# Three layer norms that leave weight and bias to the turned tiles, and 512-column up products, in a two-block transformer kernel

## The chip, the cores and the metric

The kernel runs on one core of a Trainium2 chip. The metric is the device time of one execution in microseconds (us). Times come in runs of the whole kernel; one execution was profiled, and all rows below are from it.

## The reference

Batch 1, 256 tokens, width 1024, float32. A first block (adaptive norm, a mixer of two attentions, an MLP) is followed by two layers, each of them a mixer and an MLP with a layer norm behind each:

```
x = first_block(x, c, ...)                       # its MLP: D_FF 4096, square(relu(h @ w1)) @ w2
for i in range(2):
    mix = nsa_pool_mixer(x, ...) if i == 0 else gla_mixer(x, ...)
    x = layer_norm(ALPHA * x + mix, ln1_g[i], ln1_b[i])
    x = layer_norm(ALPHA * x + square(relu(x @ w1[i])) @ w2[i], ln2_g[i], ln2_b[i])
layer_norm(x, g, b) = (x - mean) * rsqrt(var + 1e-5) * g + b      # mean and var over the 1024 channels
```

So there are three MLPs and four layer norms. The norms are numbered 0 to 3 here; norm 0 stands ahead of MLP 1, norm 1 ahead of the second layer's mixer (its input products, "C in"), norm 2 ahead of MLP 2, and norm 3 gives the output.

## The kernel before

Every weight comes from memory once, as tiles of 128 rows x 1024 numbers in six `raw` slots, in one fixed order, fetched by SyncE. For precision each weight tile is split in two: ScalarE copies it to `whi` (rounded to float32r), VectorE writes the rest, `wlo = raw - whi`; both have six slots. Activations are split the same way, `hT_hi` and `hT_lo`, `uhi` and `ulo`. Each product is made of three: hi x hi, hi x lo, lo x hi. `hi_to(s)` and `lo_to(s)` in the programs of ScalarE and VectorE mean: split the weight tiles up to s. A raw slot is free for the next fetch when `wlo` is written (`raw_done`), a split slot when TensorE has used it (`w_used`). All order on an engine is written out by hand: a wait holds everything behind it on that engine.

**Norms.** `x` is two tiles (t = 0, 1) of 128 tokens x 1024. VectorE adds the product to x in halves (`ln_half`, with `bn_stats`), then `ln_end` aggregates, hands the variance to GpSimd (`rsqrt`, a power), and meanwhile and afterwards makes two passes over each half of x: `(x - mean) * g`, then `* rstd + b`. Each half counts up `src_ready`, which releases one quarter: TensorE turns it (4 transposes of 128x128 into PSUM), ScalarE copies it to `hT_hi` (`quarter_hi`), VectorE writes `hT_lo = PSUM - hT_hi` (`quarter_lo`, `hTlo_done`), and the first products wait for that. `busy(b, n)` is n idle-time filler products on TensorE with no use for the result.

**MLP** (`mlp`, 16 steps of 256 of the 4096 inner channels). Step 0 is made with tokens as rows (`up_first`) and turned back (`turn_first`); for steps 1 to 15 `up(j)` makes 256 channels x 256 tokens in one PSUM bank: per 128 channels of the input and per 128 output channels three products of 256 columns (lines 1894 to 1896), 48 in all. Then ScalarE takes relu and its square (`uhi`), VectorE the square again and `ulo`. `down(j)` adds u x w2 to four output banks with 24 products of 512 columns (lines 1752 to 1754, the helper `three`). The order on TensorE is up(j+1), down(j). At the end it is up(14), down(13), up(15) and then the last parts of `down`.

Of the kernel before, what the change touches and what calls it, by code (L numbers as in the profile page):

```python
# [5 lines left out]
F32 = mybir.dt.float32  # L6
# [6 lines left out]
P = 128  # L13
# [157 lines left out]
def block_program(nc, dram, out):  # L171
    with ExitStack() as ctx:
# [3 lines left out]
        def sem(name):  # L176
# [7 lines left out]
        hT_hi = sb("hT_hi", [P, KC, S], F32R)  # L184
        hT_lo = sb("hT_lo", [P, KC, S], F32R)
# [11 lines left out]
        tab = sb("tab", [P, 1536])  # L197
        identb = sb("identb", [P, P], BF16)
# [10 lines left out]
        qkgain = sb("qkgain", [64, 3])  # L209
        bfor = sb("bfor", [P, 8])  # L210
# [55 lines left out]
        x_upd = sem("x_upd")  # L266

        relu_done, uhi_done, ulo_done, usq, up_mm, up_tr = [sem(n) for n in (
            "relu_done", "uhi_done", "ulo_done", "usq", "up_mm", "up_tr")]
# [46 lines left out]
        NF = len(GRP)  # L316
        S_BANK = [0, 1, 0, 1, 0, 1] + [1] * 12
# [25 lines left out]
        T_LAST = {1: T_OUT, 7: T_COUT}  # L343

# [10 lines left out]
        def _(sp):  # L355
# [53 lines left out]
            def fetch_mlp(w1, w2, s0):  # L409
# [22 lines left out]
                for k, f in enumerate([down(13, 0), down(13, 1), up(15, 0), up(15, 1),  # L432
                                       down(14, 0), down(14, 1), down(15, 0), down(15, 1)]):
                    fetch_w(s0 + MLP_TILES - 8 + k, *f)
# [30 lines left out]
        def _(pool):  # L465
# [48 lines left out]
            load_ln(0)  # L514
            rsqrt(S_N2, 1)
# [31 lines left out]
            pool.wait_ge(src_ready, units(6))  # L547
# [3 lines left out]
            pool.wait_ge(src_ready, units(7))  # L551
# [5 lines left out]
            pool.wait_ge(src_ready, units(9))  # L557
# [8 lines left out]
        def _(act):  # L566
# [31 lines left out]
            def quarter_hi(n, q):  # L598
# [3 lines left out]
                if n in T_LAST and in_hT(n, j):  # L602
                    act.wait_ge(w_used, T_LAST[n])
                nc.scalar.activation(split_dst(n, j)[0][:, :, rows_of(t)],
# [19 lines left out]
            def mlp(m, s0):  # L624
# [9 lines left out]
                def relu(j, i=None):  # L634
                    n = j0 + j
                    at = lambda v, d: v if i is None else i * d + v
                    used = s0 + (2 + 2 * j if j < 2 else 4 * j)
                    act.wait_ge(w_used, at(used, 4 * TURN))
                    if n >= 1:
                        act.wait_ge(usq, at(n, TURN))  # L640
                        act.wait_ge(uhi_done, at(n, TURN))
# [6 lines left out]
                for t in range(NT):  # L648
# [6 lines left out]
                    ins = nc.scalar.activation(pr[:, 0, t * FFB:(t + 1) * FFB], AT[:, 2 * t, 0:FFB], ACT.Relu)  # L655
                ins.then_inc(relu_done, 1)
# [3 lines left out]
                relu(1)  # L660
                with act.Fori(0, TURNS) as i:
                    for q in range(TURN):
                        for k in range(4):
                            hi(8 + 4 * q + k, i)
                        relu(2 + q, i)
                nxt[0] = s0 + MLP_TILES - 8
                hi_to(s0 + MLP_TILES - 5)
                relu(MLP_STEPS - 2)
                hi_to(s0 + MLP_TILES - 1)
                relu(MLP_STEPS - 1)  # L670
# [323 lines left out]
            for q in range(4):  # L994
                hi_to(T_CIN + 1 + q) if q in (1, 2) else None
                quarter_hi(6, q)
# [76 lines left out]
        def _(dve):  # L1073
# [66 lines left out]
            def quarter_lo(n, q):  # L1140
# [3 lines left out]
                hi, lo = split_dst(n, j)  # L1144
                tt(lo[:, :, rows_of(t)], tr_bank(n, t, j).rearrange("p (c s) -> p c s", c=4),
# [36 lines left out]
            def ln_half(n, pb, t, h, s_end):  # L1182

                product_wait(pb, t, h, s_end)
                xs = x[:, t, half(h)]
# [4 lines left out]
            def ln_end(n, t, between=None):  # L1190
# [3 lines left out]
                ts(stat[:, c:c + 1], bn[:, t, 13:14], LN_EPS, None, ALU.add).then_inc(var_ready, 1)  # L1194
                dve.wait_ge(ld_row, 32 * (n + 1))
# [7 lines left out]

            def out_norm(n, pb, s_end, stage):
# [5 lines left out]
                lo_to(s_end[1] + 1)  # L1210
                ln_end(n, 0)
# [7 lines left out]
            def mlp(m, s0):  # L1219
# [9 lines left out]
                def square(j, i=None):  # L1229
                    n = j0 + j  # L1230
                    at = lambda v: v if i is None else i * TURN + v
                    dve.wait_ge(relu_done, at(n + 1))
                    if n >= 1:
                        dve.wait_ge(ulo_done, at(n))
                    tt(pr[:, 1, :], pr[:, 0, :], pr[:, 0, :], ALU.mult).then_inc(usq, 1)  # L1235
                    dve.wait_ge(usq, at(n + 1))
                    dve.wait_ge(uhi_done, at(n + 1))
                    tt(ulo[:, j % 2, :], pr[:, 1, :], uhi[:, j % 2, :].bitcast(F32), ALU.subtract).then_inc(ulo_done, 1)
# [3 lines left out]
                dve.wait_ge(relu_done, j0 + 1)  # L1242
# [4 lines left out]
                lo_to(s0 + 7)  # L1247
                square(1)
                with dve.Fori(0, TURNS) as i:
                    for q in range(TURN):  # L1250
                        for k in range(4):
                            lo(8 + 4 * q + k, i)
                        square(2 + q, i)
                nxt[0] = raw_of(s0 + MLP_TILES - 8)
                lo_to(s0 + MLP_TILES - 5)
                square(MLP_STEPS - 2)
                lo_to(s0 + MLP_TILES - 1)
                square(MLP_STEPS - 1)
# [1245 lines left out]
```

## Time and profile before

| | |
|---|---|
| median of 3 runs | 1003.92 us (1003.64 to 1007.0) |
| profiled execution, its own time | 1002.46 us |
| its span in the profile | 1000.3 us |
| TensorE busy / VectorE busy / ScalarE busy | 965.0 / 650.7 / 465.7 us |
| mean granted TensorE clock | 0.994 |

A busy share is an average over stages. What a change is worth is read from the stretch in which it lies: in the MLP stretches TensorE has no idle time, between them it waits.

### The profile page before, as it was taken

The page shows a single profiled execution, that of the slowest core. Times are in us where ns is not written, and L with a number is a line of the kernel's source. Part 1 is how long each engine was busy: PE and PEld are TensorE (multiplying, and loading weights), DVE is VectorE, ACT ScalarE, POOL GpSimd, SP SyncE. Part 2 cuts the span into 40 slices and gives each one's busy share as a digit, 9 for nine tenths or more (in the row PEclk, how much of TensorE's full clock was granted, in tenths as well). Part 3 has the DMA queues.
Part 4 walks back from the last instruction along what each step waited for, and adds up shares of the span by engine and source line. Part 5 has one row for each costly group of instructions (what it writes and reads, how often), then busy time and mean ns, then how long its engine had stood idle before and what let it go on. Part 6 is the DMA issues. An engine that isn't in the chain of part 4 may idle for free.

```text
span 1000.3 us, 15011 instructions
## 1 busy us (share of the span) xinstructions
PE 965.0 (96%) x5664; PEld 828.0 (83%) x5664; DVE 650.7 (65%) x822; ACT 465.7 (47%) x706; POOL 53.9 (5%) x59
## 2 busy tenths in 40 slices
PE   8999999799999999999899999998999999999996
PEld 6778877699999987876699999997776889999995
DVE  5877897875554766566975545557633876555555
ACT  5576535455444444543354445434552435444540
POOL 3040101100000001000200000001000010000000
PEclk9999999999999999999999999999999999999998
DMA  9979778495566557321385565564442547565531
GB/s 309 344 226 304 233 229 274 163 330 176 170 199 202 206 190 167 122 85 53 115 262 188 195 200 174 174 200 152 127 147 85 170 133 244 192 198 199 168 126 43
DMA packets 109991, 186.94 MB, mean 187 GB/s; under 512 B 8696, under 2 KB 67088, under 8 KB 109920
## 3 DMA queue, kind: packets, MB, share of 16 engines
q1 hardware_dynamic: 104800, 177.33, 54.5%
q0 software_dynamic: 2592, 8.53, 3.0%
q8 instruction: 35, 0.57, 0.2%
q10 hardware_dynamic: 2544, 0.35, 0.2%
q14 instruction: 20, 0.16, 0.0%
HBM read 185.13 MB, written 1.05 MB: 186 GB/s over the span
## 4 chain that ended last, share of the span: by engine, by line
PE 79%; DVE 10%; ACT 3%; issue 3%; DMA 2%; POOL 2%; SPq 0%; POOLq 0%; DVEq 0%; ACTq 0%
PE PJ L1752 14%; PE PJ L1753 14%; PE PJ L1754 13%; PE AT L1896 9%; PE AT L1895 9%; PE AT L1894 9%; DVE wlo L1100 2%; POOL rstd L471 2%; PE AT L1983 1%; ACT whi L585 1%; DMA raw<-in_w_out_dram 1%; PE AT L1738 1%; DVE acc L1126 1%; PE AT L1995 1%; DVE bn L1188 1%
## 5 line engine op out<-in xcount | busy, mean ns | idle before, releaser
L1100 DVE TENSOR_TENSOR wlo<-raw,whi 128x1024 fp32r<-128x1024 f32 x144 | 172.9, 1221 | 51.5 <-ACT whi L585 50.6
L1894 PE MATMUL AT<-hT_hi,whi 128*128 128x256 f32 x720 | 203.8, 283 | 0.0
L1896 PE MATMUL AT<-hT_hi,wlo 128*128 128x256 f32 x720 | 203.7, 283 | 0.0
L1895 PE MATMUL AT<-hT_lo,whi 128*128 128x256 f32 x720 | 203.7, 283 | 0.0
L1226 DVE TENSOR_TENSOR wlo<-raw,whi 128x1024 fp32r<-128x1024 f32 x144 | 169.8, 1221 | 32.1 <-ACT whi L632 31.4
L585 ACT ACTIVATE whi<-raw 128x1024 fp32r<-128x1024 f32 x144 | 147.0, 1055 | 51.2 <-DMA raw<-in_w_in_dram 29.1
L1752 PE MATMUL PJ<-whi,uhi 128*128 128x512 f32 x432 | 170.1, 394 | 0.4 <-DVE ulo L1575 0.2
L1753 PE MATMUL PJ<-wlo,uhi 128*128 128x512 f32 x432 | 168.6, 390 | 0.0
L1754 PE MATMUL PJ<-whi,ulo 128*128 128x512 f32 x432 | 168.2, 389 | 0.0
L632 ACT ACTIVATE whi<-raw 128x1024 fp32r<-128x1024 f32 x144 | 144.3, 1049 | 47.5 <-PE PJ L1754 43.9
L1894 PEld LDWEIGHTS AT<-hT_hi,whi 128*128 128x128 f32 x720 | 138.0, 192 | 1.6
L1895 PEld LDWEIGHTS AT<-hT_lo,whi 128*128 128x128 f32 x720 | 138.0, 192 | 1.6
L1896 PEld LDWEIGHTS AT<-hT_hi,wlo 128*128 128x128 f32 x720 | 138.0, 192 | 0.0
L1235 DVE TENSOR_TENSOR pr<-pr 128x512 f32<-128x512 f32 x45 | 31.1, 691 | 162.0 <-ACT pr L642 162.0
L1752 PE MATMUL PJ<-whi,hT_hi 128*128 128x512 f32 (+1 forms) x320 | 131.3, 410 | 4.3 <-DVE hT_lo L1568 1.4
L1754 PE MATMUL PJ<-whi,hT_lo 128*128 128x512 f32 (+1 forms) x320 | 123.9, 387 | 0.0
L1753 PE MATMUL PJ<-wlo,hT_hi 128*128 128x512 f32 (+1 forms) x320 | 123.9, 387 | 0.0
L642 ACT ACTIVATE pr<-AT 128x512 f32<-128x512 f32 x45 | 26.9, 597 | 190.9 <-PE AT L1896 190.9
L1752 PEld LDWEIGHTS PJ<-whi,uhi 128*128 128x128 f32 x432 | 81.3, 188 | 17.8 <-issue 2.0
L1754 PEld LDWEIGHTS PJ<-whi,ulo 128*128 128x128 f32 x432 | 81.1, 188 | 17.4
L1753 PEld LDWEIGHTS PJ<-wlo,uhi 128*128 128x128 f32 x432 | 81.3, 188 | 15.2 <-issue 0.2
L1752 PEld LDWEIGHTS PJ<-whi,hT_hi 128*128 128x128 f32 x320 | 60.5, 189 | 22.1 <-issue 6.1
(312 smaller groups left out, 1061.5 us busy)
## 6 DMA issues: line engine op xcount, KB each, us to landing
raw<-in_mlp_w_dram SPq DMA_DIRECT2D x128, 512.0 KB, 4.9
raw<-in_w_in_dram SPq DMA_DIRECT2D x32, 512.0 KB, 6.3
raw<-in_w_ada_dram SPq DMA_DIRECT2D x32, 512.0 KB, 5.4
raw<-in_w_mlp_in_dram SPq DMA_DIRECT2D x32, 512.0 KB, 5.0
raw<-in_w_mlp_out_dram SPq DMA_DIRECT2D x32, 512.0 KB, 5.1
raw<-in_c_w_in_dram SPq DMA_DIRECT2D x24, 512.0 KB, 4.3
raw<-in_w_ada_dram SPq DMA_DIRECT2D x32, 256.0 KB, 6.4
raw<-in_a_w_in_dram SPq DMA_DIRECT2D x12, 512.0 KB, 5.2
```

Source lines behind the costliest of these rows:

```text
L585: nc.scalar.activation(whi[:, s % SPL, :], raw_slot(r), ACT.Copy).then_inc(hi_done, 1)
L632: nc.scalar.activation(whi[:, s % SPL, :], raw_slot(r), ACT.Copy).then_inc(hi_done, 1)
L642: nc.scalar.activation(pr[:, 0, :], AT[:, j % 2, :], ACT.Relu).then_inc(relu_done, 1)
L1100: tt(wlo[:, n % SPL, :], raw_slot(r), whi[:, n % SPL, :].bitcast(F32), ALU.subtract).then_inc(raw_done, 1)
L1226: tt(wlo[:, s % SPL, :], raw_slot(r), whi[:, s % SPL, :].bitcast(F32), ALU.subtract)\
L1235: tt(pr[:, 1, :], pr[:, 0, :], pr[:, 0, :], ALU.mult).then_inc(usq, 1)
L1752: mm(o, a, hi, start=start, stop=False)
L1753: mm(o, a, lo, start=False, stop=False)
L1754: return mm(o, b, hi, start=False, stop=stop)
L1894: mm(o, whi[:, s % SPL, c], hT_hi[:, k, :], start=first, stop=False, skip_group_check=True)
L1895: mm(o, whi[:, s % SPL, c], hT_lo[:, k, :], start=False, stop=False, skip_group_check=True)
L1896: ins = mm(o, wlo[:, s % SPL, c], hT_hi[:, k, :], start=False, stop=last, skip_group_check=True)
```

## The change

It has four parts.

1. **Up products.** `hT_hi` and `hT_lo` of one input channel block stand side by side, so `whi x hT_hi` and `whi x hT_lo` become one product of 512 columns, each into a half of a bank of its own; `wlo x hT_hi` stays one of 256. An `up` step now has 16 products of 512 columns and 16 of 256, and takes two banks. The two halves of a bank have to be added: ScalarE copies the one out, VectorE adds the other, then takes relu times itself, ScalarE copies the result to `uhi`, VectorE makes `ulo`. One weight tile's `wlo` (11+4q) moves into the middle of that. Step 15's u goes into a free part of `hT`, and the order at the end is up(14), up(15), down(13).
2. **Norms 0 to 2.** VectorE makes one pass over a half: `(x - mean) * rstd`, then `src_ready`. Weight and bias are put on by ScalarE from the turned tile, where a channel is a partition: four activations of 128x128 with scale and bias by partition, into `sc`, and then the rounding copy to `hT_hi`. VectorE subtracts from `sc`.
3. **x itself** still needs weight and bias for the next residual: `affine`, two passes over each of the four halves (8 instructions on VectorE for each norm), behind `square(1)` of MLP 1 and 2 and among the first C-in tiles.
4. **Small orders.** GpSimd loads the three weights and biases by channel (`lncol`, six transfers of 1024 single numbers) ahead of `rsqrt(S_N2)`; fillers ahead of MLP 1 and 2 go from 1+2+4 to 1+2, at C in by one each; the weight splits T_CIN+2 and +3 stand at other places.

```diff
-        hT_hi = sb("hT_hi", [P, KC, S], F32R)
-        hT_lo = sb("hT_lo", [P, KC, S], F32R)
+        hT = sb("hT", [P, KC, 2, S], F32R)
+        hT_hi, hT_lo = hT[:, :, 0, :], hT[:, :, 1, :]
...
             load_ln(0)
+            for n in range(3):
+                g, b = (("ln1_g_2", "ln1_b_2"), ("ln2_g_2", "ln2_b_2"))[n % 2]
+                for i, v in enumerate((g, b)):
+                    pool.dma_start(lncol[:, 2 * n + i, :], dram[v][n // 2].rearrange("(k p) -> p k", p=P),
+                                   allow_slow_non_contiguous=True).then_inc(ld_col, 16)
             rsqrt(S_N2, 1)
...
+                if n in LN_STAGE:
+                    act.wait_ge(ld_col, 96)
+                    if q >= 2:
+                        act.wait_ge(hTlo_done, units(n) + q - 1)
+                    for c in range(4):
+                        ins = nc.scalar.activation(turned_y(q)[:, c, :], tr_bank(n, t, j)[:, c * P:(c + 1) * P], ACT.Identity,
+                                                   scale=lncol[...], bias=lncol[...])
+                    link(ins)
+                    nc.scalar.activation(split_dst(n, j)[0][:, :, rows_of(t)], turned_y(q), ACT.Copy).then_inc(hThi_done, 1)
+                    return
...
-                    nc.scalar.activation(pr[:, 0, :], AT[:, j % 2, :], ACT.Relu).then_inc(relu_done, 1)
-                    act.wait_ge(relu_done, at(n + 1, TURN))
-                    nc.scalar.activation(uhi[:, j % 2, :], pr[:, 0, :], ACT.Square).then_inc(uhi_done, 1)
+                    nc.scalar.activation(pr[:, 0, :]..., AT[:, up_banks(j), S:], ACT.Copy).then_inc(cross_out, 1)
+                    act.wait_ge(usq, at(n + 1, TURN))
+                    nc.scalar.activation(u_slot(j)[0], blocks4(pr[:, 1, :]), ACT.Copy).then_inc(uhi_done, 1)
...
+                if n < 3:
+                    between()
+                    rstd_wait()
+                    for j in range(2):
+                        xs = x[:, t, half(j)]
+                        ts(xs, xs, bn[:, t, 12:13], rstd[:, c:c + 1], ALU.subtract, ALU.mult).then_inc(src_ready, 1)
+                    return
...
+            def affine(n, stage, t, j):
+                dve.wait_ge(ld_row, 32 * (n + 1))
+                dve.wait_ge(tr_done, units(stage) + 2 * t + j + 1)
+                xs = x[:, t, half(j)]
+                link(tt(xs, xs, rows[:, 0, half(j)], ALU.mult))
+                tt(xs, xs, rows[:, 1, half(j)], ALU.add).then_inc(x_new, 1)
...
+                    z = pr[:, 0, :].rearrange("p (f s) -> p f s", f=2)
+                    tt(z, AT[:, up_banks(j), 0:S], z, ALU.add).then_inc(up_out, 1)
+                    dve.wait_ge(up_out, at(n + 1, TURN))
+                    stt(pr[:, 1, :], pr[:, 0, :], 0.0, pr[:, 0, :], ALU.max, ALU.mult).then_inc(usq, 1)
+                    between() if between else None
...
-            lo_to(T_CIN + 1)
-            for t in range(NT):
-                ln_half(1, B_MLP1, t, 0, (T_CIN, T_CIN))
-                ln_half(1, B_MLP1, t, 1, (T_CIN, T_CIN))
-                lo_to(T_CIN + 3) if t else None
-                ln_end(1, t)
-                quarter_lo(6, 2 * t)
-                quarter_lo(6, 2 * t + 1)
-                lo_to(T_CIN + 2)
+            lo_to(T_CIN)
+            ln_half(1, B_MLP1, 0, 0, s_end)
+            ln_half(1, B_MLP1, 0, 1, s_end)
+            ln_end(1, 0, lambda: lo_to(T_CIN + 1))
+            ln_half(1, B_MLP1, 1, 0, s_end)
+            quarter_lo(6, 0)
+            quarter_lo(6, 1)
+            ln_half(1, B_MLP1, 1, 1, s_end)
+            ln_end(1, 1, lambda: lo_to(T_CIN + 2))
+            lo_to(T_CIN + 3)
+            quarter_lo(6, 2)
+            quarter_lo(6, 3)
...
-                                mm(o, whi[:, s % SPL, c], hT_hi[:, k, :], start=first, stop=False, skip_group_check=True)
-                                mm(o, whi[:, s % SPL, c], hT_lo[:, k, :], start=False, stop=False, skip_group_check=True)
-                                ins = mm(o, wlo[:, s % SPL, c], hT_hi[:, k, :], start=False, stop=last,
+                                mm(o, whi[:, s % SPL, c], hT[:, k, :, :].rearrange("p a s -> p (a s)"),
+                                   start=k == 0, stop=False, skip_group_check=True)
+                                ins = mm(o[:, 0:S], wlo[:, s % SPL, c], hT_hi[:, k, :], start=False, stop=k == KC - 1,
                                          skip_group_check=True)
```

## Rows read from the trace of the kernel before

**Rows 1.** The page: the shares of the chain that ended last, by engine.

```profile
PE 79%; DVE 10%; ACT 3%; issue 3%; DMA 2%; POOL 2%; SPq 0%; POOLq 0%; DVEq 0%; ACTq 0%
```

**Rows 2.** Busy time by stretch: length, PE, PEld, DVE, ACT, POOL, clock, DMA.

```profile
418.00:421.50 3.50, 3.50 (x11) 2.69 (x11) 1.78 (x5) 1.91 (x9) 0.00 (x0) 0.59 0.13 49
...
516.00:666.00 150.00, 150.00 (x973) 137.55 (x972) 82.25 (x81) 67.86 (x79) 0.00 (x0) 1.00 0.60 198
```

**Rows 3.** Timeline of TensorE, one step of MLP 1: start, duration, line, shape.

```profile
560.16 0.28 PE L1894 MATMUL AT<-hT_hi,whi 128*128 128x256 f32 x1
...
565.91 0.40 PE L1752 MATMUL PJ<-whi,uhi 128*128 128x512 f32 x1
...
571.38 0.28 PE L1894 MATMUL AT<-hT_hi,whi 128*128 128x256 f32 x1
```

**Rows 4.** Groups by line and form: count, busy us, mean ns, idle before.

```profile
L644 ACT ACTIVATE uhi<-pr 128x512 fp32r<-128x512 f32 x45 | 28.6, 634 | 1.4
L604 ACT ACTIVATE hT_hi<-AT 128x512 fp32r<-128x512 f32 x24 | 13.9, 596 | 67.5 <-PE AT L1738 67.5
L655 ACT ACTIVATE pr<-AT 128x256 f32<-128x256 f32 x6 | 2.3, 381 | 6.7 <-PE AT L1754 6.7
...
L1180 DVE TENSOR_TENSOR x<-x,sc 128x512 f32<-128x512 f32 x8 | 5.5, 692 | 0.3
L1119 DVE TENSOR_SCALAR prT<-raw,cvec 128x512 f32<-128x512 f32 x3 | 1.4, 479 | 0.0
```

**Rows 5.** Timeline of VectorE and TensorE, norm 0 to MLP 1.

```profile
496.80 0.75 DVE L1201 SCALAR_TENSOR_TENSOR x<-x,rstd,rows 128x512 f32<-128x512 f32 x1 [0.52 <-POOL rstd L471]
...
497.61 0.66 PE L1738 MATMUL AT<-cst,x 128*128 128x128 f32 x4 [0.26 <-DVE x L1201]
...
499.74 0.60 PE L1738 MATMUL AT<-cst,x 128*128 128x128 f32 x4
...
501.79 0.35 PE L1752 MATMUL AT<-whi,hT_hi 128*128 128x256 f32 x1
...
503.30 0.28 PE L1894 MATMUL AT<-hT_hi,whi 128*128 128x256 f32 x1
...
509.72 0.47 PE L1752 MATMUL PJ<-whi,uhi 128*128 128x512 f32 x1
```

**Rows 6.** Timeline of ScalarE: activations with scale and bias by partition.

```profile
16.66 0.60 ACT L709 ACTIVATE hT_hi<-qT,modc 128x256 fp32r<-128x256 f32 x1
17.17 0.58 ACT L712 ACTIVATE pr<-qT,modc 128x256 f32<-128x256 f32 x1
```

**Rows 7.** Timeline of TensorE and VectorE, norm 2 to MLP 2.

```profile
819.57 0.60 PE L1873 MATMUL AT<-cst,pr 128*128 128x128 f32 x4
...
823.11 0.47 PE L1752 MATMUL PJ<-whi,uhi 128*128 128x512 f32 x1
...
827.65 4.62 DVE L1226 TENSOR_TENSOR wlo<-raw,whi 128x1024 fp32r<-128x1024 f32 x4
```

**Rows 8.** Timeline of VectorE and TensorE, norm 1 to C in.

```profile
681.63 0.68 DVE L1186 SCALAR_TENSOR_TENSOR x<-x,PJ 128x512 f32<-128x512 f32 x1
...
684.52 1.23 DVE L1100 TENSOR_TENSOR wlo<-raw,whi 128x1024 fp32r<-128x1024 f32 x1
...
677.11 0.66 PE L1738 MATMUL AT<-cst,x 128*128 128x128 f32 x4 [1.19 <-DVE x L1201]
...
681.80 0.58 PE L1752 MATMUL PJ<-whi,hT_hi 128*128 128x512 f32 x1
...
690.23 0.58 PE L1752 MATMUL PJ<-whi,hT_hi 128*128 128x512 f32 x1
```

**Rows 9.** Timeline of GpSimd; and a step of the chain that ended last.

```profile
181.10 1.48 POOL L471 TENSOR_TENSOR rstd<-stat,nhalf 128x1 f32<-128x1 f32 x1 [16.10 <-DVE stat L1157]
...
379.86 1.68 POOL L528 DMA_DIRECT2D acc<-in_a_cmp_pos_dram  x1
...
164.28 8.67 DMA raw<-in_w_out_dram
```

More of the change, by code:

```diff
@@ L550, in _ @@
                 rsqrt(S_LN + 2 + t, 1)
[L551 removed]
+            pool.wait_ge(x_new, 8)
             load_ln(2)
@@ L659, in mlp @@
                 hi_to(s0 + 7)
-                relu(1)
+                square_hi(1)
                 with act.Fori(0, TURNS) as i:
@@ L1246, in mlp @@
                 tt(ulo[:, 0, :], AT[:, 3, :], uhi[:, 0, :].bitcast(F32), ALU.subtract).then_inc(ulo_done, 1)
-                lo_to(s0 + 7)
-                square(1)
+                lo_to(s0 + 6)
+                square(1, between=lambda: lo_to(s0 + 7))
+                for t in range(NT):
+                    for j in range(2):
+                        affine(*((0, 5), (2, 8))[m - 1], t, j) if m else None
                 with dve.Fori(0, TURNS) as i:
                     for q in range(TURN):
-                        for k in range(4):
+                        for k in range(3):
                             lo(8 + 4 * q + k, i)
-                        square(2 + q, i)
+                        square(2 + q, i, lambda: lo(11 + 4 * q, i))
                 nxt[0] = raw_of(s0 + MLP_TILES - 8)
-                lo_to(s0 + MLP_TILES - 5)
-                square(MLP_STEPS - 2)
+                lo_to(s0 + MLP_TILES - 7)
+                square(MLP_STEPS - 2, between=lambda: lo_to(s0 + MLP_TILES - 6))
+                lo_to(s0 + MLP_TILES - 4)
+                square(MLP_STEPS - 1, between=lambda: lo_to(s0 + MLP_TILES - 3))
                 lo_to(s0 + MLP_TILES - 1)
-                square(MLP_STEPS - 1)
             nc.vector.memset(rows[:, 0, 0:S], 0.0).then_inc(zeroed, 1)
@@ L1900, in down_part @@
                 def down_part(j, s, f, t, h, first=False, last=False):
-                    c = slice(f * S + t * P, f * S + (t + 1) * P)
+                    hi, low = u_slot(j)
                     w = slice(512 * h, 512 * (h + 1))
-                    return three(bank(pb + h, t), uhi[:, j % 2, c], ulo[:, j % 2, c], whi[:, s % SPL, w],
+                    return three(bank(pb + h, t), hi[:, 2 * f + t, :], low[:, 2 * f + t, :], whi[:, s % SPL, w],
                                  wlo[:, s % SPL, w], first, last)
@@ L1919, in down @@
                         ins.then_inc(w_used, 1)
+                transposes(stage, 1, src)
                 busy(3, 1) if m else None
-                transposes(stage, 1, src)
+                up_first(0, 0)
                 busy(3, 2) if m else None
-                up_first(0, 0)
-                busy(3, 4) if m else None
                 transposes(stage, 2, src)
@@ L1938, in mlp @@
                 up(14, 54)
-                down(13, 56)
-                up(15, 58)
+                up(15, 56)
+                down(13, 58)
                 if spare:
+                    pe.wait_ge(up_out, j0 + MLP_STEPS - 1)
                     spare()
```

88 lines of the change are left out of this document (49 added, 39 removed).

## The prediction

> **What bounds the kernel now.** I read the page first, then busy time by stretch, then timelines where TensorE waits. The chain that ended last is TensorE for 79% [rows 1]. In a stretch of MLP 1, TensorE is busy 150.00 of 150.00 us; VectorE has 82 and ScalarE 68 [rows 2]. So inside the three MLPs only TensorE's own work counts. Ahead of MLP 1, of C in and of MLP 2 it waits for a serial chain: VectorE norms a half, TensorE turns it, ScalarE rounds it, VectorE makes the low part. There, latencies count.
>
> **Up products.** From 560.16 to 565.91 run the 48 products of an up step, 0.1198 us each; from 565.91 to 571.38 the 24 of a down step, 0.2279 us each [rows 3]. At 2.4 GHz 256 columns last 0.1067 us and 512 last 0.2133, so each product pays some 0.013 us beside its columns. The new step has 16 of either: 16 x (0.2279 + 0.1198) = 5.56 us against 5.75, 0.187 less. The shape of 512 is at hand in `down`, from the same kind of operand, so I take its spacing. Bounds: no gain, if the joined product costs two of 256 (0.2396); 0.21 per step, if it saves one whole overhead of 0.013. 42 steps (j = 2 to 15) stand in TensorE's unbroken stream: **-7.9 us**. Step 1 of each MLP is left out, for a wait behind it decides (below).
>
> The Trainium skill (TensorE: Matmul & The Clock Gate, Back-to-back issue gap) gives columns/2.4 plus only 2.5 ns. The rows disagree: 0.1198 and 0.2279 us. By the page's figure the 42 steps would save an estimated 1.7 us.
>
> The longer way to u is covered. Behind up(j): copy out 0.60, add 0.69, relu times itself 0.69, copy 0.63, subtract 0.69 [rows 4], with one weight split of 1.2 in it: some 5 us. `down(j)` starts only after down(j-1) and up(j+1), 5.47 + 5.56 = 11.0 us later. VectorE's step grows from 6.0 to 6.7 us of 11.0, ScalarE's hardly. If that cover were gone, each step would pay the excess. The new order at the end hides step 15's chain under down(13); it was hidden before.
>
> **The norm's release.** Before, two passes a half. Now VectorE restarts at the same place after GpSimd (496.80, [rows 5]), with one pass of 0.48 (L1119, [rows 4]; upper bound 0.75, L1201 [rows 5]). The quarter is released 0.25 us earlier, and the fourth, which waited for two more passes, some 2 us earlier.
>
> **The price in ScalarE.** `quarter_hi` was one copy of 0.60 (L604). Now four activations, 128 columns, two per-partition operands. With 256 columns these start 0.51 us apart [rows 6]; 256 columns less cost 0.596 - 0.381 = 0.215 us [rows 4], 128 columns 0.11. So 0.40 apart, 1.7 us for four, then a rounding copy of 0.63 (L644): 2.3 us, **1.7 more per quarter**. Bounds: 0.9 more, if the operands cost nothing (0.381 - 0.107 for one, overlapped by 0.08), and 2.0, if they don't overlap. ScalarE takes quarters in turn, so a second one follows 2.3 us behind the first.
>
> *Norm 0 to MLP 1.* The first half: released 0.27 us earlier, 1.7 us longer on ScalarE. VectorE waits for it with `quarter_lo(0)` ahead of the second half's sums; that uses up the gain of the passes, and the second variance is out at the same time as before. Third quarter: VectorE's pass 496.80 to 497.28, turned at 497.36, low part done near 501.1. The fourth is turned by 500 but queues on ScalarE: 2.3 us later. Before, turned at 499.74, used at 501.79, 2.05 us [rows 5]. Now `up_first(1, 1)` starts at 497.36 + 2.1 + 1.7 + 2.2 = 503.4, 1.6 later. The wait behind `turn_first` (819.57 to 823.11 in MLP 2, 3.54 us [rows 7]) hangs on the middle of up(1), now at 2.78 rather than 2.88 us: down(0) comes **1.5 us later** than 509.72. The fewer fillers cost and give nothing: TensorE would have waited.
>
> *Norm 2 to MLP 2.* The same, but VectorE here ran `lo_to` (1.2 us) before the first variance and now runs it under GpSimd's power: 0.7 us off the start. **0.8 us later.**
>
> *Norm 1 to C in.* VectorE drops one weight split ahead of the first sums: variance 0.64 earlier, first transposes at 676.2 instead of 677.11, the second quarter right behind, TensorE ready at 679.3. First quarter's low part: first product at 680.0 against 681.80 [rows 8]. But T_CIN+2's split, done by 681.63 before [rows 8], now stands behind both quarters' low parts, the sums of the second half (half of 681.63 to 684.52, 1.44 us [rows 8]) and the variance: second quarter rounded at 681.4, low part 682.2, sums 683.5, split 683.8 to 685.1. TensorE has used T_CIN and +1 by 682.7 and **waits 2.4 us**. T_CIN+3 follows at 687.2, and t = 0 ends near 688.6. Only then are the last quarters turned; from there 2.05 + 1.7 us: second tile at 692.3 against 690.23. **2.1 us later.** Nothing behind gives it back, for TensorE is the bound there too.
>
> **`affine`.** 8 passes of 0.69 (L1180, [rows 4]), pairs of 1.33: 5.3 us a norm. At C in there is room between splits. In MLP 1 and 2 they stand ahead of tile 8's split, behind `square(1)`: that was at 827.65 [rows 7], 4.54 us after down(0)'s start; now it is square 0.6 us later, and 5.3: 10.5 us after, done at 11.7. TensorE needs it after down(0) and up(2), 5.57 + 5.56 = 11.1. **Stall 0.7 us, twice** (0 to 1.5).
>
> **GpSimd.** Six more transfers ahead of a power that waited 16.10 us for its operand [rows 9]. One with 4096 single numbers took 1.68 us to issue [rows 9]; six with 1024 at 0.5 to 1.7 are 3 to 10 us, hidden. They share the DMA engines with a weight tile that is on the chain with 8.67 us (from 164.28, [rows 9]). Between 0 and 1.6 us; I take 0.2.
>
> **Sum.** -7.9 + 1.5 + 0.8 + 2.1 + 1.4 + 0.2 = -1.9 us. Against the profiled execution's 1002.46 that is 1000.6; the median of the runs lies 1.46 above it, so I predict **1002.0**.
>
> **Rivals.** (A) *The turned tiles are as quick as before.* Operands by partition cost little, and C in's split order costs less than I think. For it: without a price for the operands a quarter is longer by 0.9 us only, and the release is up to 2 us earlier. Against: the spacing with operands [rows 6]. The transitions then cost some 1 us in all, stalls included: -7, 997.0.
>
> (B) *The joined products give nothing or little.* A 512-column product into an AT bank, between two of 256, could cost two of them, by its weight load. Against: `down` shows 0.2279 with a load each. The sum becomes +6.0, 1009.9: slower. It passes +5 us once the joined product costs over 0.238 us. By the Trainium skill's 2.5 ns (same page and section) an estimate is +4.3, just short of that.
>
> (C) *The clock falls.* From 418.0 to 421.5 the granted clock was 0.59 on average [rows 2], so a part of it ran at 1.2 GHz instead of 2.4; such a dip costs a busy TensorE 3.5 x 0.41 = 1.4 us. C in gets waits of 2.4 and 2.3 us within 10 us of each other. Two dips more: 1004.8. Against: the waits before, up to 1.19 us [rows 8], brought none there. [...]
>
> (D) *The small loads delay the weight tile* by the whole 1.6 us: 1003.4.
>
> **Chances.** Forecast 0.48, A 0.30, B 0.08, C 0.09, D 0.05. A measurement here tells 0.5% (5 us) from no change. Faster by over that, below 998.9: most of A, a little of the forecast, 0.30. Slower, above 1008.9: B and a tail, 0.10. Within: 0.60. The forecast's own bounds (quarters 0.9 to 2.0, stalls 0 to 1.5, loads 0 to 1.6) give 998 to 1006; with A, 995.5 to 1006.5.
>
> **What would show it.** Right: up steps of 5.56 us, steps of 11.03 us, TensorE still without idle in the MLPs; ScalarE's four activations 0.4 us apart; `up_first(1, 1)` waiting for ScalarE; at C in a wait of 2.4 us for VectorE's `wlo`; 0.7 us ahead of down(1). Wrong: another spacing of the joined product, quarters of 1.5 us on ScalarE, or waits inside the loops, where VectorE or a weight fetch comes late.

## The result: 6 us slower

The changed kernel takes 1011.16 us (median of 6 runs, 1010.37 to 1014.59) against 1004.97 for the kernel before (6 runs): a ratio of 1.0065 with a 95% interval of 1.0049 to 1.0081, so 4.9 to 8.1 us slower. I had predicted 1002.0.

The execution profiled is the slowest of the six, 1014.59 us with a span of 1012.8. The page of after has these rows, the chain's shares among them (that of before in [rows 1]):

```profile
PE 967.6 (96%) x4924; PEld 793.3 (78%) x4924; DVE 675.7 (67%) x879; ACT 479.4 (47%) x754; POOL 60.1 (6%) x65
...
PE 74%; DVE 10%; ACT 5%; DMA 5%; issue 4%; POOL 2%; SPq 0%; POOLq 0%; DVEq 0%; ACTq 0%
```

TensorE's share of the chain fell from 79 to 74%, and the DMA's rose from 2 to 5%, for which my sum had no more than the 0.2 us of the small loads.

**A step of MLP 1**, on the timeline of after (start, duration, line, shape), against [rows 3]:

```profile
569.94 0.39 PE L1947 MATMUL AT<-hT,whi 128*128 128x512 f32 x1
...
570.28 0.40 PE L1947 MATMUL AT<-hT,whi 128*128 128x512 f32 x1
570.51 0.28 PE L1949 MATMUL AT<-hT,wlo 128*128 128x256 f32 x1
570.63 0.40 PE L1947 MATMUL AT<-hT,whi 128*128 128x512 f32 x1
570.87 0.28 PE L1949 MATMUL AT<-hT,wlo 128*128 128x256 f32 x1
570.99 0.40 PE L1947 MATMUL AT<-hT,whi 128*128 128x512 f32 x1
...
575.58 0.40 PE L1809 MATMUL PJ<-whi,uhi 128*128 128x512 f32 x1
```

The up step lasts 575.58 - 569.94 = 5.64 us, not 5.56: 0.11 less than before, where I had 0.187. From a joined product to the start of the product of 256 behind it are 0.23 to 0.24 us (0.2358 on the mean of the 212 pairs between 529 and 684 us), from a product of 256 to the next joined one 0.117.

**Norm 0 to MLP 1**, against [rows 5]: timeline of ScalarE and TensorE.

```profile
499.35 1.50 ACT L623 ACTIVATE sc<-AT,lncol 128x128 f32<-128x128 f32 x4 [5.90 <-PE AT L1795]
...
500.88 0.63 ACT L627 ACTIVATE hT<-sc 128x512 fp32r<-128x512 f32 x1
...
501.42 1.49 ACT L623 ACTIVATE sc<-AT,lncol 128x128 f32<-128x128 f32 x4
...
519.31 0.48 PE L1809 MATMUL PJ<-whi,uhi 128*128 128x512 f32 x1 [0.16 <-issue]
...
531.05 0.50 PE L1809 MATMUL PJ<-whi,uhi 128*128 128x512 f32 x1 [0.36 <-DVE wlo L1268]
```

A quarter occupies ScalarE for 2.07 us (499.35 to 501.42; I had 2.3). down(0) starts at 519.31, 9.59 us after its place before. The norm's first transposes were 8.24 late already, so the norm itself costs 1.35 us. At down(1) TensorE waits for the weight tile that stands behind `affine`; the wait and its after-effect make some 0.6 us (see `affine` in the table of terms).

**Norm 1 to C in**, against [rows 8]: TensorE's first transposes and its waits.

```profile
685.36 1.11 PE L1795 MATMUL AT<-cst,x 128*128 128x128 f32 x8 [0.77 <-DVE x L1228]
694.04 0.47 PE L1809 MATMUL PJ<-whi,hT 128*128 128x512 f32 x1 [1.92 <-DVE wlo L1124]
696.52 0.50 PE L1809 MATMUL PJ<-whi,hT 128*128 128x512 f32 x1 [0.86 <-DVE wlo L1124]
701.69 0.47 PE L1809 MATMUL PJ<-whi,hT 128*128 128x512 f32 x1 [2.21 <-DVE hT L1170]
```

Here are the waits that I had drawn: 1.92 us for the third weight tile (I had 2.4), 2.21 for the last quarters (I had 2.3).

**The small loads.** GpSimd's timeline, and the piece of the chain that ended last which answers to [rows 9]:

```profile
168.61 0.92 POOL L527 DMA_DIRECT2D lncol<-in_ln_g_dram  x1
...
173.01 0.88 POOL L527 DMA_DIRECT2D lncol<-in_ln_b_dram  x1
...
169.03 14.56 DMA raw<-in_w_mlp_in_dram
```

Six issues of 0.9 us, and a weight tile that is on the chain for 14.56 us. The tile on the chain before, with 8.67, was another; but the four tiles `raw<-in_w_mlp_in` issued between 150 and 195 us land after a median of 14.7 us here and of 9.6 before.

### The profile page after: what moved, and what is told of

It reads as the page before. It is cut to its first block, busy times and chain, and to the rows that moved or that the text cites. A ratio compares the mean times of both kernels' runs of the same rounds, so it can differ in the third digit from the quotient of the medians.

```text
span 1012.8 us, 13660 instructions
## 1 busy us (share of the span) xinstructions
PE 967.6 (96%) x4924; PEld 793.3 (78%) x4924; DVE 675.7 (67%) x879; ACT 479.4 (47%) x754; POOL 60.1 (6%) x65
## 4 chain that ended last, share of the span: by engine, by line
PE 74%; DVE 10%; ACT 5%; DMA 5%; issue 4%; POOL 2%; SPq 0%; POOLq 0%; DVEq 0%; ACTq 0%
PE AT L1947 16%; PE PJ L1809 14%; PE PJ L1810 13%; PE PJ L1811 13%; PE AT L1949 8%; DVE wlo L1124 2%; DMA raw<-in_w_in_dram 2%; POOL rstd L480 2%; DMA raw<-in_w_mlp_in_dram 1%; PE AT L2036 1%; ACT sc L623 1%; ACT whi L599 1%; PE AT L1795 1%; DVE acc L1150 1%; PE AT L2048 1%
## 5 line engine op out<-in xcount | busy, mean ns | idle before, releaser
L1947 PE MATMUL AT<-hT,whi 128*128 128x512 f32 x720 | 256.2, 398 | 0.0
L1949 PE MATMUL AT<-hT,wlo 128*128 128x256 f32 x720 | 202.1, 281 | 0.0
L1947 PEld LDWEIGHTS AT<-hT,whi 128*128 128x128 f32 x720 | 135.3, 188 | 32.8
L1810 PE MATMUL PJ<-wlo,uhi 128*128 128x512 f32 x408 | 159.2, 390 | 0.0
L1809 PE MATMUL PJ<-whi,hT 128*128 128x512 f32 (+1 forms) x344 | 144.2, 419 | 14.4 <-DVE wlo L1124 6.2
L1278 DVE TENSOR_TENSOR pr<-AT,pr 128x512 f32<-128x512 f32 x45 | 31.1, 690 | 160.8 <-ACT pr L665 160.8
L1949 PEld LDWEIGHTS AT<-hT,wlo 128*128 128x128 f32 x720 | 136.0, 189 | 1.5
L1810 PE MATMUL PJ<-wlo,hT 128*128 128x512 f32 (+1 forms) x344 | 136.4, 396 | 0.0
L1811 PE MATMUL PJ<-whi,hT 128*128 128x512 f32 (+1 forms) x344 | 136.1, 396 | 0.0
L1809 PEld LDWEIGHTS PJ<-whi,hT 128*128 128x128 f32 x344 | 67.2, 195 | 35.2 <-issue 11.5
L1811 PEld LDWEIGHTS PJ<-whi,hT 128*128 128x128 f32 x344 | 67.0, 195 | 14.3
L1810 PEld LDWEIGHTS PJ<-wlo,hT 128*128 128x128 f32 x344 | 67.3, 196 | 13.0 <-issue 1.0
```

Source lines behind the costliest of these rows:

```text
L1278: tt(z, AT[:, up_banks(j), 0:S], z, ALU.add).then_inc(up_out, 1)
L1809: mm(o, a, hi, start=start, stop=False)
L1810: mm(o, a, lo, start=False, stop=False)
L1811: return mm(o, b, hi, start=False, stop=stop)
L1947: mm(o, whi[:, s % SPL, c], hT[:, k, :, :].rearrange("p a s -> p (a s)"), start=k == 0, stop=False, skip_group_check=True)
L1949: ins = mm(o[:, 0:S], wlo[:, s % SPL, c], hT_hi[:, k, :], start=False, stop=k == KC - 1, skip_group_check=True)
```

## Where the time went, by stretch

The groups that the helper `transposes` makes on TensorE, and the turns of `turn_first`, are the same in all kernels, so the starts of their first products cut each profile into like stretches (us; each is a difference of two starts, and the last ends with TensorE's last product). Transposes by other lines are no landmarks. "Before" was profiled three times.

| stretch | before, 3 profiles | after |
|---|---|---|
| start to the first group of transposes | 135.01, 136.61, 136.06 | 138.64 |
| to MLP 0's first transposes | 48.42, 48.44, 48.80 | 52.16 |
| to MLP 0's turn | 15.44, 15.45, 15.83 | 16.94 |
| MLP 0, from its turn | 171.30, 171.30, 171.31 | 169.75 |
| second attention | 120.25, 121.93, 118.75 | 121.16 |
| norm 0 to its turn | 15.77, 15.75, 15.75 | 17.12 |
| MLP 1, to C in's transposes | 170.93, 170.92, 170.92 | 169.59 |
| C in, to the helper's next group | 100.66, 100.67, 100.65 | 105.38 |
| to MLP 2's turn | 41.80, 41.80, 41.79 | 42.22 |
| MLP 2 to the end | 171.40, 171.38, 171.38 | 170.48 |

The MLPs and the norms repeat within 0.02 us. In the first 200 us and in the second attention the same kernel scatters by up to 3 us, since the granted clock falls at changing places. Two such places of after, in the view of busy time by stretch (columns as in [rows 2]):

```profile
418.00:425.00 7.00, 7.00 (x46) 6.60 (x46) 2.36 (x4) 3.39 (x12) 0.00 (x0) 0.76 0.54 148
...
701.00:708.00 7.00, 6.31 (x21) 5.06 (x22) 5.34 (x7) 4.69 (x8) 0.00 (x0) 0.76 0.25 72
```

A mean of 0.76 over 7 us is 7 x 0.24 x 2 = 3.4 us at 1.2 GHz, and costs a busy TensorE 1.7 us. The first lies in the second attention, where before has one as well [rows 2]; the second, in C in, is in none of the three profiles of before. (I had priced such a fall at 1.4 us, from a window that began 0.6 us inside it.) The profile that I predicted from has the shortest start of the three.

## The experiments

**1. The loads moved behind; the loads alone.** The first takes the changed kernel and issues the six loads later on GpSimd's queue:

```diff
             load_ln(0)
-            for n in range(3): ... pool.dma_start(lncol[:, 2 * n + i, :], ...)
             rsqrt(S_N2, 1)
...
+            for n in range(3): ... pool.dma_start(lncol[:, 2 * n + i, :], ...)
             for t in range(NT):
                 rsqrt(S_LN + t, 1)
```

> The changed kernel with its six loads of lncol issued behind GpSimd's loads for the second attention (near 380 us, used from 490 us). Theory 1 (the six loads at 168 to 174 us hold up a weight tile, 3.8 us of TensorE's time): 3.8 us less than the changed kernel, so 1007.4, 2.4 us above before; the weight tiles raw<-w_mlp_in land in some 9.6 us as before, not 14.7. Rival (the 3.8 us between 165 and 183 us is the scatter of one execution, such as a dip of the clock): no change, 1011.2, 6.2 above before.

The second adds the `+` lines to the kernel before, between `load_ln(0)` and `rsqrt(S_N2, 1)`:

> The kernel before, with the six loads of lncol added at the changed kernel's place, into a tile that nothing reads. Theory 1: 3.8 us above before, 1008.8, all of it between 165 and 183 us. Rival: within 0.5 us of before.

Measured: 1009.21 us (12 runs; ratio to before 1.0043, 1.0024 to 1.0062) and 1007.47 us (12 runs; 1.0029, 1.0012 to 1.0046). So the loads alone cost the kernel before 1.2 to 4.6 us (theory 1 had 3.8), and moving them gave 2 us. The transfers of 170 to 180 us, by slices of 0.25 us, in before, then in the kernel before with the loads:

```profile
GB/s 328 344 295 320 291 287 246 352 324 348 328 361 389 385 389 381 377 369 393 369 401 320 381 361 365 389 397 356 410 373 356 369 352 393 406 340 410 352 442 365
```

```profile
DMA  9998998999999999999999499668999999999899
GB/s 344 401 442 328 385 451 360 459 401 393 426 401 393 401 385 340 300 252 106 74 66 33 45 34 62 72 131 170 204 154 183 129 168 137 183 214 247 246 303 307
```

The rate falls from some 370 to between 33 and 215 GB/s for over 4 us, while the engines' busy share (the digits, in tenths) is under 0.8 in three slices only. The loads are 96 packets of 256 bytes in this trace, beside 96 of 4 bytes. From 174 to 179.5 us a packet of 256 bytes took 0.32 us on the mean, where one of 4096 took 0.16, and the weight tiles' packets of 1024 took 0.094 us instead of the 0.049 that they take in before from 170 to 173 us. The stretch from 165 to 183 us lasted 18.6 to 18.9 us in nine of the ten profiles without the loads at that place (19.6 in the tenth) and 20.7, 21.0 and 21.1 with them (22.3 in that of after, where the clock stood at 1.2 GHz for some of it): 2.2 us. The 20.99 among them had the clock down for its last 1.1 us only, so the 2.2 us are not the clock's; the rest of theory 1's 3.8 us goes with the fall in after's profile, as its rival had it. The Trainium skill (DMA: Bandwidth & Descriptors, Rules for kernel authors) says that a last dimension that isn't contiguous becomes one descriptor per element. The trace agrees in that 24 KB cost the others so much, but it records packets and not descriptors, and no run loads the same 24 KB contiguously: that single numbers are the reason, and not six more small loads, is argued.

**2. The product alone; the MLPs alone.** The changed kernel with the joined product taken apart:

```diff
-  mm(o, whi[:, s % SPL, c], hT[:, k, :, :].rearrange("p a s -> p (a s)"), start=k == 0, ...)
+  mm(o[:, 0:S], whi[:, s % SPL, c], hT_hi[:, k, :], start=k == 0, stop=False, ...)
+  mm(o[:, S:], whi[:, s % SPL, c], hT_lo[:, k, :], start=False, stop=k == KC - 1, ...)
```

> The changed kernel with each joined product of 512 columns taken apart into two of 256 into the two halves of the same bank; nothing else differs. Theory 2 (the joined product has a spacing of 0.236 us, so a step gains 0.11 us): 45 steps of 0.11, 5 us above the changed kernel, 1016.1. Rival (my forecast, 0.187 a step, the rest being a disturbance of one execution): 8.4 us above it. Second rival (the joined product gains nothing): the same time.

The other way round, the MLPs of after in the kernel before:

```diff
 # from the changed kernel: hT, up_banks, u_slot, square_hi, square, up, down_part, the order at the end
 # from the kernel before: ln_end, out_norm, quarter_hi, quarter_lo, C in, the fillers; no affine, no lncol
```

> The kernel before with the MLPs of the changed one: the joined products, the longer way to u, the new order at the end; the three norms, their quarters, the loads and the fillers as before. Theory 2: 5 us under before, 1000.0, since nothing but the steps of 0.11 us remains. Rival (0.187 a step): 8 us under it, 997. Second rival (the longer way to u costs waits of its own in the MLPs): at or above before.

Measured: 1014.11 us (1.0091, 1.0065 to 1.0117) and 1005.39 us (12 runs; 0.9999, 0.9980 to 1.0017). In the profiles the joined products are worth what theory 2 says: with them apart, MLP 0 lasts 171.33 us against 169.75; the MLPs alone in the kernel before last 169.81, 169.03 and 169.83, 4.9 us less in all. Of the 1.9 us in MLP 1, 0.33 is not TensorE's work: from its last product to the next transposes are 1.25 us instead of 1.58. But the time of that kernel didn't fall by 5 us, and the split one rose by 3 only. Something outside the MLPs took 2 to 5 us back in the kernels that have the joined products. One piece is in the profile of the MLPs alone: a fall of the clock in C in, 101.92 us instead of 100.66.

**3. Two more profiles of before, to know the scatter.**

> The kernel before itself, for one more profile of it. The execution first profiled showed two falls of the granted clock beside the one at its end, and a mean of 0.994; the mean over 29 executions is 0.989. Theory 3 (falls at changing places in the first 200 us belong to every execution and not to an edit): four to six falls here, the first transposes of 165 us some 2 to 5 us later than in the first profile, and from 205 us on the same lengths of every stretch within 0.1 us, one fall near 418 us apart. Rival (the edits bring the early falls): as in the first profile, two.

> The same once more: the scatter of the first 200 us between two executions of one kernel on one chip. Theory 3: up to 4 us between the two; the stretch from 165 to 183 us within 1 us of 18.55 us in both, since no small loads are there.

Measured: 1005.75 and 1002.73 us, spans 1003.6 and 1000.6; the clock fell four times in the one and twice in the other, beside the fall at the end. Every stretch behind 205 us but the second attention repeats (table above). The scatter of falls is real, but the first stretch of after is longer than all three.

**4. Joined products in groups.** In the kernel of the MLPs alone, one weight tile's products in two groups:

```diff
+                        for part in range(2):
                             for kk in range(4):
                                 for f in range(2):
...
+                                    if part == 0:
                                         mm(o, whi[:, s % SPL, c], hT[:, k, :, :]...)
+                                    else:
                                         ins = mm(o[:, 0:S], wlo[:, s % SPL, c], hT_hi[:, k, :]...)
```

> The MLPs of the changed kernel in the kernel before, with the products of each weight tile in two groups: its eight joined products of 512 columns first, then its eight of 256 columns. Theory 2a (the joined product's 0.236 us comes from the alternation of 512 and 256 columns): 0.227 and 0.120 us, 5.55 us a step, 0.09 us less than in the changed kernel, 45 steps: 4 us under the alternating form. Rival (it is the joined product's operands or its bank): 0.236 us as before, and then 5.64 us a step; if the spacing of the 256 rises from 0.117 to 0.120 as well, 5.7 us.

Measured: 998.24 us; 0.9943, 0.9923 to 0.9963. Timeline of one step (a row with x8 is eight in a row):

```profile
603.47 1.98 PE L1905 MATMUL AT<-hT,whi 128*128 128x512 f32 x8
...
605.28 1.11 PE L1908 MATMUL AT<-hT,wlo 128*128 128x256 f32 x8
606.23 2.00 PE L1905 MATMUL AT<-hT,whi 128*128 128x512 f32 x8
608.07 1.12 PE L1908 MATMUL AT<-hT,wlo 128*128 128x256 f32 x8
609.03 0.40 PE L1764 MATMUL PJ<-whi,uhi 128*128 128x512 f32 x1
```

609.03 - 603.47 = 5.56 us, to the hundredth what I had predicted for the changed kernel. The same product with the same operands into the same bank is 0.227 to 0.229 us behind another of 512 columns. Theory 2a holds: the alternation costs 0.008 us a joined product and gives 0.003 back on the product of 256. Against the alternating form of experiment 2 the MLP stretches are 3.4 us shorter (168.65, 168.00 and 168.67 us); the two kernels' ratios lie 5.6 us apart, and the rest is outside the MLPs.

The grouped order also changes the bank at every product, which the alternating one doesn't. That is not the reason: three products in a row go into one bank in `down`, at 0.228, and in before's `up`, at 0.120. And a single change of size costs nothing in sum. In before, the first product of a `down` (512 behind 256 columns) takes 0.233 us in all 13 cases between 520 and 660 us, and the first of an `up` (256 behind 512) takes 0.113: 0.006 more and 0.007 less. In the grouped kernel a product of 512 that has one of 512 in front takes 0.227 also where one of 256 follows. So it is not what follows that sets the spacing, and only the strict alternation leaves 0.006 us a pair.

**5. The third weight tile at C in.** First, in the kernel of experiment 1 (loads behind), its low part under GpSimd's power:

```diff
-            hi_to(T_CIN + 1)
+            hi_to(T_CIN + 2)
...
-            lo_to(T_CIN)
+            lo_to(T_CIN + 1)
...
-            ln_end(1, 0, lambda: lo_to(T_CIN + 1))
+            ln_end(1, 0, lambda: lo_to(T_CIN + 2))
...
-            ln_end(1, 1, lambda: lo_to(T_CIN + 2))
-            lo_to(T_CIN + 3)
+            ln_end(1, 1, lambda: lo_to(T_CIN + 3))
```

> The changed kernel with the six loads behind and, at C in, the third weight tile split ahead of the first quarters: ScalarE rounds it before the first quarter, VectorE makes its low part under GpSimd's first power, the fourth tile's under the second power. Theory 4 (TensorE's wait of 2.0 us there hangs on that split): the wait for wlo goes from 2.8 us to under 1, the variance of the first half is 0.64 us later, and from the first transposes to the end of C in the stretch is 1.5 to 2 us shorter than the 3.1 us more than before. Rival (the second quarters decide, so that the gain is given back there): 0.5 us or less.

Measured: 1009.10 us (one run). C in is 2.57 us shorter than with the loads behind alone (101.21 against 103.78), but MLP 1's stretch 2.16 longer (171.77 against 169.61): 0.41 in all, the rival. The timeline shows why:

```profile
681.19 1.06 ACT L599 ACTIVATE whi<-raw 128x1024 fp32r<-128x1024 f32 x1 [6.27 <-PE PJ L1810]
682.28 1.22 DVE L1124 TENSOR_TENSOR wlo<-raw,whi 128x1024 fp32r<-128x1024 f32 x1 [2.33 <-ACT whi L599]
683.42 1.00 DVE L1228 TENSOR_SCALAR x<-x,bn,rstd 128x512 f32<-128x512 f32 x2
684.02 1.11 PE L1794 MATMUL AT<-cst,x 128*128 128x128 f32 x8 [2.93 <-DVE x L1228]
```

ScalarE can round that tile only when TensorE lets go of its slot (six tiles back), at 681.19. VectorE had nothing else to go on with, and the norm's passes stood behind. The wait moved from behind the transposes to ahead of them.

So the low part belongs where VectorE is idle anyway, between the second half's first sums and the first quarter. The changed kernel with the loads behind, the groups of experiment 4, and:

```diff
-            hi_to(T_CIN + 1)
+            hi_to(T_CIN + 2)
...
             ln_half(1, B_MLP1, 1, 0, s_end)
+            lo_to(T_CIN + 2)
             quarter_lo(6, 0)
...
-            ln_end(1, 1, lambda: lo_to(T_CIN + 2))
-            lo_to(T_CIN + 3)
+            ln_end(1, 1, lambda: lo_to(T_CIN + 3))
```

> The changed kernel with three of its costs mended: the six loads behind, the up products in groups of eight of 512 and eight of 256 columns, and at C in the third weight tile rounded before the first quarter, with its low part made between the second half's first sums and the first quarter's low part, where VectorE stood idle for 1.25 us. Sum of the measured parts: loads -2.3, groups -1.1 in MLP 0 and 1 and -1.2 in MLP 2, C in -2.0 (TensorE's wait for wlo gone, the first transposes not later): 7.6 under the changed kernel, 1003.6, 1 us under before. Rival (at C in a wait only moves, as when the low part stood under GpSimd's power): 0.4 there, 1005.2.

Measured: 1002.50 us; 0.9967, 0.9954 to 0.9980. Its waits in C in:

```profile
688.09 0.50 PE L1809 MATMUL PJ<-whi,hT 128*128 128x512 f32 x1 [0.55 <-DVE wlo L1124]
693.26 0.47 PE L1809 MATMUL PJ<-whi,hT 128*128 128x512 f32 x1 [2.21 <-DVE hT L1170]
```

The 1.92 and 0.86 us for the weight tile have become 0.55; C in lasts 101.20 us, 0.5 more than before instead of 3.1 (MLP 1's stretch is not longer, so this time no wait has moved there). The 2.21 us behind the last quarters stay.

**6. The first 135 us.** The kernel before and the one with the MLPs alone have the same code up to 190 us. Beside the clock's falls one thing differed there, and it is the same in after. The transfers from 20 to 30 us, by slices of 0.25 us, in before and in after:

```profile
GB/s 348 361 340 352 344 344 352 344 356 340 315 270 187 236 178 257 332 349 369 369 344 254 262 295 287 316 270 279 299 352 389 385 373 377 381 385 369 401 381 373
```

```profile
GB/s 340 340 356 356 336 352 352 344 344 361 300 300 146 71 28 7 9 27 77 147 168 166 168 150 182 160 272 295 354 385 336 304 275 303 336 373 369 385 377 410
```

At 23.5 to 24.5 us nearly nothing moves in after. The hole is in all six profiles whose third part of the page counts 31 fetches of instructions, and in none of those with 35 or more. It isn't the edit's lines: the kernel with the joined product taken apart (same MLPs, 35 fetches) has no hole. The page of after, then of that kernel:

```profile
q8 instruction: 31, 0.51, 0.2%
```

```profile
q8 instruction: 35, 0.57, 0.2%
```

Joined products make TensorE's program shorter. To lengthen it without other work, the loops of the MLPs are written out:

```diff
-TURN = 6
-TURNS = 2
+TURN = 12
+TURNS = 1
```

In the grouped kernel of experiment 4:

> The kernel before with grouped MLP products, its MLP loops of two turns of six steps written out in full (one turn of twelve): the same work and order, more code to fetch. All profiles with the joined products fetched 31 blocks of 16 KB of instructions over the span and show transfers at 15 to 60 KB per us near 23 us, where the profiles with single products (35 blocks) show 170 to 210; the first transposes of 135 us come at 137.0 to 140.6 us with it and at 135.0 to 137.4 without. Theory 5 (the hole hangs on the length or the place of the program): more blocks, and a rate near 23 us that is no longer under 100; start to first transposes 135 to 137 us; the time 0 to 3 us under the looped form, 997. Rival (it hangs on the joined products or hT themselves): the hole stays, 998. In either, the MLP stretches of 168.65, 168.0 and 168.7 us don't move by over 0.2, unless fetching more code holds TensorE up.

In the changed kernel, and as a control in the kernel before:

> The changed kernel with its MLP loops written out in full (one turn of twelve steps), nothing else. Theory 5 (the changed kernel's shorter program brings a hole in the transfers near 23 us, 2 to 3 us to the first transposes): no hole, first transposes at 135 to 137.4 us rather than 138.6, the time 2 to 3 us less, 1008.5, 3.5 us above before. Rival (the hole costs nothing of its own; what looked so was the scatter of the clock's falls): 1011.2.

> The control: the kernel before with its MLP loops written out in full. It has no hole to lose. Theory 5: within 0.5 us of before, 1004.8. Rival (writing out saves or costs by itself, by branches or by fetching): the MLP stretches of 171.30, 170.93 and 171.40 us change, and the time with them, by 1 us or more.

Measured: 995.69 us (0.9906, 0.9878 to 0.9934), 1006.50 (12 runs; 1.0034, 1.0014 to 1.0054) and 1006.12 (12 runs; 1.0017, 1.0002 to 1.0032). All three are without the hole (their lowest slices between 20 and 30 us are 196, 132 and 136 GB/s); this is the grouped kernel's:

```profile
GB/s 352 348 332 365 356 328 356 356 336 348 325 196 226 231 229 247 329 365 373 345 369 344 369 336 324 336 369 365 320 299 385 385 356 352 299 344 303 324 279 299
```

Both kernels with joined products gained by it, 0.9943 - 0.9906 and 1.0065 - 1.0034 of before's time, 3.7 and 3.1 us. The intervals overlap in both pairs, so this is likely and not proven. The control lost 1.7 us by its ratio (1.2 by the medians), with its MLP stretches unchanged (171.30, 170.94, 171.38), which neither side of my expectation had. From the start to the first transposes the six profiles with the hole took 137.03 to 140.60 us, mean 139.4, and the eight without 135.01 to 137.84, mean 136.5: 2.9 us.

Most of that goes with the clock. In this stretch the six profiles with the hole spent 10.7 us on the mean at 1.2 GHz, the eight without 6.2, which is worth 2.2 us to a busy TensorE. Three profiles have the same falls there, one of 6.8 us near 15 us and no other: the grouped kernel's, with the hole, took 137.03, and those of before (second) and of the changed kernel written out, without, took 136.61 and 135.85. So 0.4 to 1.2 us are left for the hole itself, and whether it brings the further falls no run shows. What in the shorter program makes the hole, its length or the place that something gets by it, is not settled: writing out changes both.

## Why the prediction was wrong

The terms, predicted and measured (stretches of the profiles against before's):

| term | predicted | measured | read from |
|---|---|---|---|
| up products | -7.9 | -4.6 | MLPs alone, to the last product: 1.5 + 1.55 + 1.55 |
| norm 0 to MLP 1 | +1.5 | +1.35 | 17.12 - 15.77 |
| norm 2 to MLP 2 | +0.8 | +0.4 | 42.22 - 41.80 |
| norm 1 to C in | +2.1 | +2.7 | 103.78 - 100.66, loads behind, less 0.42 of head start |
| `affine` | +1.4 | +1.3 | 0.66 in MLP 1, to the last product; 170.47 - 169.83 in MLP 2 |
| small loads | +0.2 | +2.2 | experiment 1 |
| start of the program, clock's falls included | none | +2.9 | experiment 6 |
| sum | -1.9 | +6.2 | measured +6.2 |

The sum's agreement is closer than its terms deserve: the last carries an uncertainty of over 1 us, and falls of the clock outside the start are in no row. A part of the miss was in the base as well: I started from 1003.92, the median of three executions, and six gave 1004.97.

**The step that failed first** is the joined product's price, the first and largest term of the sum. I took 0.2279 + 0.1198 us "from the same kind of operand", out of a stretch where products of 512 columns follow each other, and the change makes them alternate with products of 256. The pair takes 0.353 us instead of 0.348. The mechanism stood, the price was mis-sized: a step gained 0.11 us and not 0.187, which is 3.3 us of the 8.1 by which the sum was off, and experiment 4 gives the 0.187 back by the order alone. Of rival B (nothing gained) little is left: a joined product costs 0.2358 in the alternating order, just short of the 0.238 from which I had let it decide, but the products of 256 beside it came 0.003 sooner. That B's time, 1009.9, lies nearest to the measured one is chance: the products did gain, and misses of which it says nothing made up for that. The Trainium skill's 2.5 ns per product (TensorE: Matmul & The Clock Gate, Back-to-back issue gap), which that section gives for a product by itself, fits neither order here: 227 and 120 ns are some 13 ns over the columns' time.

**The small loads** were priced by their issue, and beside the weight tile I took 0.2 out of 0 to 1.6. I went by bytes and issue; 6144 single numbers are 24 KB, and over four microseconds in which the transfer engines moved little more than half of their usual rate or less. Rival D's mechanism was real beside the other misses, and its 1.6 too small.

**The start** was in no term, since no line that runs there does other work. That is the step "all else as before", which the text didn't even write down. It is also the least certain one, as most of it goes with the clock.

**C in** was right in its waits and wrong in its head start. I let the variance come 0.64 us earlier, for a weight split that VectorE drops, and the first transposes 0.91. Counted from TensorE's last product of MLP 1 the variance did come 0.62 us earlier (it starts 1.19 us ahead of that product, not 0.57), though VectorE now waited 0.76 us for TensorE ahead of the sums. But GpSimd's power took 1.47 us beside a split, not 0.99, and the transposes came only 0.42 us earlier (1.16 us behind that product, not 1.58). That is 0.5 of the 0.6 us by which C in cost more than I said.

**Right** were the norm's price, quarters of 2.1 us on ScalarE, the waits and their releasers at C in, the place of `affine`'s stall, and the MLPs otherwise without idle time. Rival A (turned tiles as quick as before) fell with the 1.35 us. Rival C (the clock) had a larger part than its chance of 0.09: the mean granted clock of the six runs of after is 0.986, of 29 of before 0.989. In those 29, 0.001 of clock goes with 0.56 us of time, so an estimate of the difference's share is 1.6 us. One fall was inside C in, as I had feared, and not in this profile alone. Four profiles have this order of waits at C in. With the loads behind there was no fall (103.78 us), but there was one with the product taken apart (104.36) and in after (105.38), and two in a row in the changed kernel written out (105.42), here in the view of busy time by stretch, where the clock is the third number from the end:

```profile
686.00:696.00 10.00, 7.83 (x25) 5.69 (x26) 2.83 (x4) 3.65 (x10) 0.23 (x1) 0.66 0.36 106
```

The mean of the four is 4.1 us above before, where the table has 3.1 ahead of the head start. Of the eight profiles with before's own C in, only that of the MLPs alone had a fall there, and the two with the third weight tile mended had none. So few profiles make it likely, not shown, that the waits at C in bring the falls. The other falls lie in the first 200 us and the second attention, where before has them too, and how many of those belong to the edit is open; the MLPs alone came out 2 us above their sum, which more falls would explain (their mean clock is 0.986 as well).

**What remains of the change:** the norms cost some 6 us and give nothing back that the runs show; mended, they still cost 3.5 (1.3, 0.5, 0.4 and 1.3 of `affine`, by the stretches; by the ratios of the mended kernel and of that of experiment 4, 2.4). The up products are the gain, if grouped. The version to keep is the kernel before with grouped products and its loops written out: 995.69 us, 0.7 to 1.2% under before.

## What to carry to other kernels

Take an instruction's price from a stretch with the same neighbours, not only the same shape: what stood around a product set its spacing here. Don't price a load by single numbers from its bytes or its issue time, and issue it where no tile on the path is in flight. An edit that makes a program shorter or longer can move time where nothing was edited, so profile the kernel before more than once, and compare by stretches between landmarks that both kernels have.

## What the runs showed of the hardware

- Products of 512 columns are 0.227 us apart behind each other. Behind one of 256 a product of 512 takes 0.233, and 0.236 where the two alternate. Products of 256 are 0.120 us apart behind each other; behind one of 512 they take 0.113, and 0.117 where the two alternate.
- GpSimd's power of one number a partition takes 0.56 us when VectorE waits, 1.0 beside a norm's pass and 1.47 beside a weight split. Two rows of the kernel after, from norm 0 and from C in:

```profile
497.45 0.56 POOL L480 TENSOR_TENSOR rstd<-stat,nhalf 128x1 f32<-128x1 f32 x1 [107.82 <-DVE stat L1222]
...
683.25 1.47 POOL L480 TENSOR_TENSOR rstd<-stat,nhalf 128x1 f32<-128x1 f32 x1 [152.01 <-DVE stat L1222]
```

  The Trainium skill (SBUF — State Buffer, Who interferes with whom) says that a VectorE instruction with two inputs from SBUF contends with a GpSimd instruction that reads SBUF, over a pair of ports that only one of them holds at a time. The trace agrees: the pass and the split both have two such inputs, and in either case the power ends 0.42 us behind the end of VectorE's instruction. So a split put under the power to hide it makes the power 0.9 us longer.
- The transfers' hole of 1.5 us near 23 us comes and goes with the program's size (31 fetches of instructions, or 35 to 45), at equal work. Why is open.
